# Attention value product: two passes with high and low value parts in one stationary block, instead of three

## The reference, cut to what matters

```python
def one_block(qi):                       # per block of 128 queries
    s = jnp.einsum('bqhd,bkhd->bhqk', qi, k).astype(jnp.float32) * scale
    p = jax.nn.softmax(s, axis=-1).astype(v.dtype)
    return jnp.einsum('bhqk,bkhd->bqhd', p, v)
```

## Time and profile before

| | |
|---|---|
| median of 3 runs | 3137.64 us (3137.29 to 3138.24) |
| the profiled execution's own time | 3137.54 us |
| its span, first to last instruction | 3135.4 us |
| TensorE busy | 3018.9 us (96%), 19892 matmuls |
| VectorE busy | 2122.9 us (68%) |
| ScalarE busy | 1141.8 us (36%) |
| mean granted TensorE clock | 0.982 of full speed |
| attention stages | about 774 to 1057 and 2280 to 2563 us |

### The profile page before, as it was taken

One profiled execution on the slowest core, in us unless ns is written; L12 is line 12 of the kernel. 1 busy time (PEld: TensorE's weight loads), 2 busy tenths in 40 slices (PEclk: granted clock), 3 DMA queues, 4 the chain that ended last, 5 costly groups with the idle time before them and its releaser, 6 DMA issues.

```text
span 3135.4 us, 48664 instructions
## 1 busy us (share of the span) xinstructions
PE 3018.9 (96%) x19892; PEld 2938.2 (94%) x19892; DVE 2122.9 (68%) x3521; ACT 1141.8 (36%) x1820; POOL 85.8 (3%) x164
## 2 busy tenths in 40 slices
PE   7999999998999999999999999999899999999998
PEld 4899999997899999999999999999789999999998
DVE  7666666646655557988968988863565556785675
ACT  3422312422444433434343433442154443443432
POOL 0000000000000000000000000000000000000000
PEclk8999999999999999999999999999999999999999
DMA  8255553345122532444322434334521242122222
GB/s 304 91 202 228 213 190 135 115 153 221 67 75 85 192 112 80 135 141 142 122 95 94 149 121 142 108 114 163 224 82 71 76 186 108 68 95 81 95 68 75
DMA packets 89743, 408.90 MB, mean 130 GB/s; under 512 B 10049, under 2 KB 13569, under 8 KB 68914
## 3 DMA queue, kind: packets, MB, share of 16 engines
q1 hardware_dynamic: 60384, 285.76, 25.6%
q0 software_dynamic: 19872, 94.53, 8.3%
q10 hardware_dynamic: 9266, 25.50, 2.2%
HBM read 359.46 MB, written 46.30 MB: 129 GB/s over the span
## 4 chain that ended last, share of the span: by engine, by line
PE 77%; DVE 14%; ACT 4%; issue 3%; DMA 1%; ACTq 0%; DVEq 0%
PE tile_psum L743 21%; PE misc_psum L860 12%; PE tile_psum L750 11%; PE misc_psum L864 6%; PE tile_psum L1215 6%; PE tile_psum L704 3%; PE tile_psum L1219 3%; PE misc_psum L669 3%; PE tile_psum L669 2%; PE tile_psum L860 2%; PE tile_psum L709 2%; PE tile_psum L1080 1%; DVE h L2254 1%; DVE wlo L2083 1%; PE tile_psum L864 1%
## 5 line engine op out<-in xcount | busy, mean ns | idle before, releaser
L743 PE MATMUL tile_psum<-n_hi,whi 128*128 128x320 f32 x1536 | 352.3, 311 | 4.0 <-issue 2.2
L743 PE MATMUL tile_psum<-n_lo,whi 128*128 128x320 f32 x1536 | 350.1, 309 | 0.0
L2083 DVE TENSOR_TENSOR wlo<-raw,whi 128x2048 fp32r<-128x2048 f32 (+4 forms) x130 | 250.6, 1930 | 114.2 <-ACT whi L1491 112.2
L743 PE MATMUL tile_psum<-x_hi,whi 128*128 128x320 f32 x1300 | 300.1, 312 | 17.4 <-DVE h L2254 11.7
L743 PE MATMUL tile_psum<-x_lo,whi 128*128 128x320 f32 x1300 | 298.3, 311 | 0.0
L743 PEld LDWEIGHTS tile_psum<-n_hi,whi 128*128 128x128 f32 x1536 | 257.6, 189 | 6.8 <-DVE n_lo L2174 4.2
L743 PEld LDWEIGHTS tile_psum<-n_lo,whi 128*128 128x128 f32 x1536 | 258.2, 189 | 0.0
L1491 ACT ACTIVATE whi<-raw 128x2048 fp32r<-128x2048 f32 (+4 forms) x130 | 208.9, 1616 | 126.7 <-DMA raw<-in_w_down 43.7
L1215 PE MATMUL tile_psum<-n_hi,whi 128*128 128x320 f32 x768 | 237.4, 320 | 11.0 <-ACT gate_out L1978 10.3
L2254 DVE SCALAR_TENSOR_TENSOR h<-tile_psum,ada_t,h 128x320 f32<-128x320 f32 (+2 forms) x408 | 154.2, 434 | 129.2 <-PE tile_psum L750 127.5
L750 PE MATMUL tile_psum<-n_hi,wlo 128*128 128x320 f32 x1536 | 241.3, 309 | 0.0
(11 more groups left out here) (384 smaller groups left out, 6450.1 us busy)
## 6 DMA issues: line engine op xcount, KB each, us to landing
w_ada<-in_w_ada POOLq DMA_DIRECT2D x72, 512.0 KB, 4.0
raw<-in_w_up SPq DMA_DIRECT2D x72, 512.0 KB, 3.8
raw<-in_w_up SPq DMA_DIRECT2D x34, 1024.0 KB, 4.9
w_ada<-in_w_ada SPq DMA_DIRECT2D x56, 512.0 KB, 6.3
raw<-in_w_gate SPq DMA_DIRECT2D x24, 1024.0 KB, 4.9
raw<-in_w_down SPq DMA_DIRECT2D x29, 768.0 KB, 4.4
whi<-table_keep SPq DMA_DIRECT2D x20, 1024.0 KB, 4.7
wlo<-table_keep SPq DMA_DIRECT2D x20, 1024.0 KB, 6.9
```

Source lines behind the costliest of these rows:

```text
L743: pe.matmul(tps[:, t.s, m, 0:TH], blk(p, m * n + k)[0], (hi, lo)[b][:, k, tok], start=k == 0 and b == 0, stop=False)
L2083: ins = dve.tensor_tensor(lo_at(r, n)[:, 0:w], raw_at(r, n)[:, 0:w], hi_at(h_, n)[:, 0:w].bitcast(F32), ALU.subtract)
```

## The change

The values are laid out in one tile `v_parts`, for each key tile as four blocks of 64 columns: high of the even head, low of the even head, low of the odd head, high of the odd head. ScalarE and VectorE each write them with two operations of 384 columns instead of one of 768, and VectorE starts after both of ScalarE's. The stationary block of a P is one head's high and low block side by side (128 columns). Two passes follow, one with the high and one with the low part of the probabilities. The result's 64 rows of the high values and 64 rows of the low values have to be added: ScalarE copies the low values' rows to `x_raw` (which lies where `x_lo` lies), moved to the other half of the partitions, VectorE adds the other rows from PSUM, frees the tile, waits for its own write and signals. The split into `x_hi` and `x_lo` is a new entry X h, one step later, at the end of step 5h+7; the last one, X7, ends the list. TensorE waits for `x_split` ahead of the projection. The product now also holds low x low.

```diff
--- before.py
+++ after.py
@@ -266,8 +266,11 @@
             order += [("T", n - 2)] + [("F", 0)] * (n != 2)
             if n % 5 == 1:
                 order += [("P", (n - 2) // 5)]
+            elif n % 5 == 2 and n > 5:
+                order.append(("X", n // 5 - 1))
         if n % 10 == 1 and n < 5 * HEADS:
             order.append(("V", n // 10))
+    order.append(("X", HEADS - 1))
     done, first, fills, out, busy = {}, {}, HYENA_FILLS, [], []
     for at, (what, n) in enumerate(order):
         if what == "F":
@@ -445,7 +448,9 @@
         (krt0,), _ = place(XL, ("k_rope_tmp", [P, TL], F32))
 
         (pth, ptl), _ = place(base, ("probs_t_hi", [P, 5, TL], F32R), ("probs_t_lo", [P, 5, TL], F32R))
-        (vh, vl, krt), _ = place(SM0, ("v_hi", [P, KEYS], F32R), ("v_lo", [P, KEYS], F32R), ("q_rope_tmp", [P, TL], F32))
+        (vals2, krt), _ = place(SM0, ("v_parts", [P, KEYS // P, 4, VD], F32R), ("q_rope_tmp", [P, TL], F32))
+        v_at = [[vals2[:, :, b, :].rearrange("p (a k) v -> p a k v", a=2) for b in bs] for bs in ((0, 3), (1, 2))]
+        (xraw,), _ = place(XL, ("x_raw", [P, 8, T], F32))
         (kh, kl, kh1, kl1, pm, qf, ckh, ckl), end4 = place(
             A0, ("k_hi", [P, KEYS], F32R), ("k_lo", [P, KEYS], F32R), ("k_hi1", [P, KEYS], F32R), ("k_lo1", [P, KEYS], F32R),
             ("probs", [P, 2, T], F32), ("q_f32", [P, T], F32), ("ckv_hi", [P, KEYS], F32R), ("ckv_lo", [P, KEYS], F32R))
@@ -509,6 +514,10 @@
 
             return halves(p) if qt < 4 else p[:, 0:TC]
 
+        def v_psum(m, e):
+
+            return mps[:, m.s, :, 0:KEYS // 2].rearrange("p a (k e v) -> p a k e v", k=3, e=2)[:, :, :, e, :]
+
         def smat(ap, at, n=P):
             return ap[:, at:at + n]
 
@@ -517,6 +526,7 @@
         hi_ready, lo_ready = sem("panel_hi_ready"), sem("panel_lo_ready")
         early_in, piece_in = [sem(f"ada_early_in{k}") for k in range(4)], [sem(f"ada_rows_in{k}") for k in range(2)]
         cols_in, cols_on, turned_out, w3_in = sem("c_cols_in"), sem("c_cols_silu"), sem("ada_turned"), [sem(f"w3_in{l}") for l in range(DEPTH)]
+        x_half, x_sum, x_split, low_values = sem("x_half_out"), sem("x_summed"), sem("x_split"), sem("low_values_part")
         ada_late = [sem(f"ada_late_in{k}") for k in range(2)]
         ada_in, ada_used = [sem(f"ada_in{k}") for k in range(2)], sem("ada_used")
         ada_half = sem("ada_half_done")
@@ -1283,16 +1293,19 @@
                         for t in (turned, vals):
                             pe.wait_ge(t.free, t.free_at)
                         t = taken(slots.head_tile())
+                        both = [vals2[:, kt, n % 2 * 2:n % 2 * 2 + 2, :].rearrange("p b v -> p (b v)") for kt in range(6)]
                         for kt in range(5):
-                            kk = slice((kt + 1) * P, (kt + 2) * P)
-                            mm3([tps[:, t.s, 0, :]], (vh[:, kk], vl[:, kk]), [(pth[:, kt, :], ptl[:, kt, :])], kt == 0, kt == 4)
-                        mm3([tps[:, t.s, 1, 0:TC]], (vh[:, 0:TC], vl[:, 0:TC]), [(pch[:, :], pcl[:, :])], True, True)\
-                            .then_inc(t.done, 1)
+                            for x_ in (pth, ptl):
+                                pe.matmul(tps[:, t.s, 0, :], both[kt + 1], x_[:, kt, :], start=kt == 0 and x_ is pth, stop=kt == 4 and x_ is ptl)
+                        for x_ in (pch, pcl):
+                            ins = pe.matmul(tps[:, t.s, 1, 0:TC], both[0], x_[:, :], start=x_ is pch, stop=x_ is pcl)
+                        ins.then_inc(t.done, 1)
                     elif what == "F":
                         part_of_gate(n)
 
 
                 all_read(tile_free)
+                pe.wait_ge(x_split, HEADS * (l + 1))
                 pe.wait_ge(fill_free, 48 * (l + 1))
                 for m in range(KT):
                     if m % 2 == 0:
@@ -2023,7 +2036,8 @@
                             act.activation(kl1[ROPE_AT[1], :], kl[ROPE_AT[0], :].bitcast(F32), ACT.Copy).then_inc(keys_turned, 1)
                     elif what == "V":
                         m = misc()
-                        split_hi(halves(vh[:, :]), mps[:, m.s, :, 0:KEYS // 2])
+                        for e in range(2):
+                            split_hi(v_at[0][e], v_psum(m, e))
                     elif what == "S":
                         m = misc()
                         c = n % 3
@@ -2039,7 +2053,12 @@
                     elif what == "P":
                         t = seen(slots.head_tile())
                         rows = slice((n % 2) * VD, (n % 2 + 1) * VD)
-                        split_hi(xh[rows, 2 + n // 2, :], flat(tps, t.s)[rows, 0:T])
+                        other = slice((1 - n % 2) * VD, (2 - n % 2) * VD)
+                        act.activation(xraw[rows, 2 + n // 2, :], flat(tps, t.s)[other, 0:T], ACT.Copy).then_inc(x_half, 1)
+                    elif what == "X":
+                        rows = slice((n % 2) * VD, (n % 2 + 1) * VD)
+                        act.wait_ge(x_sum, due(x_sum))
+                        split_hi(xh[rows, 2 + n // 2, :], xraw[rows, 2 + n // 2, :])
                     elif what == "F":
                         after_fill(n)
 
@@ -2881,7 +2900,9 @@
                         lo_part(ql[ROWS[n % 2], n % 2, :], qf[ROWS[n % 2], :], qh[ROWS[n % 2], n % 2, :], q_split)
                     elif what == "V":
                         m = misc()
-                        lo_part(halves(vl[:, :]), mps[:, m.s, :, 0:KEYS // 2], halves(vh[:, :]), m.free)
+                        dve.wait_ge(op_hi, due.now(op_hi) + 2)
+                        for e in range(2):
+                            lo_part(v_at[1][e], v_psum(m, e), v_at[0][e], (low_values, m.free)[e])
                     elif what == "S":
                         scored[n] = m = misc()
                         own(dve.tensor_reduce(stat[:, c:c + 1], scores(m.s, qt), AX.XY if qt < 4 else AX.X, ALU.max))
@@ -2904,7 +2925,14 @@
                     elif what == "P":
                         t = seen(slots.head_tile())
                         rows = slice((n % 2) * VD, (n % 2 + 1) * VD)
-                        lo_part(xl[rows, 2 + n // 2, :], flat(tps, t.s)[rows, 0:T], xh[rows, 2 + n // 2, :], t.free)
+                        dve.wait_ge(x_half, due(x_half))
+                        y = xraw[rows, 2 + n // 2, :]
+                        dve.tensor_tensor(y, y, flat(tps, t.s)[rows, 0:T], ALU.add).then_inc(t.free, 1)
+                        dve.wait_ge(t.free, t.free_at)
+                        dve.sem_inc(x_sum, 1)
+                    elif what == "X":
+                        rows = slice((n % 2) * VD, (n % 2 + 1) * VD)
+                        lo_part(xl[rows, 2 + n // 2, :], xraw[rows, 2 + n // 2, :], xh[rows, 2 + n // 2, :], x_split)
                 dve.sem_inc(heads_done, 1)
                 for m in range(KT):
                     dve.wait_ge(gate_on, due(gate_on))
```

## The result

The changed kernel takes 3143.22 us (median of 20 runs, 3138.86 to 3149.39), the one before 3137.27 in its 20 runs beside it. The ratio is 1.0022, interval [1.0015, 1.0029]: 6.9 us slower by the ratio, 6.0 by the two medians, where I had forecast no change, 3137.6. The time lies in the range (3125 to 3144), but outside the forecast case (3132 to 3142), and the interval excludes 1. The profiled execution took 3142.65 us, its span is 3140.4.

What follows compares the result with a forecast made beforehand. TensorE was taken as the bound, busy nearly all of the span. Removed matmuls -19.8, stage end +3.4, queue stalls +13.4 and clock +3.0 summed to 0.0 us: forecast 3137.6 us, no change, range 3125 to 3144.

Steps and rivals of the forecast that it cites:

- forecast case: Whole kernel: likeliest case, no change at 3137.6 us, own range 3132 to 3142; chance 0.44.
- Removed matmuls, -19.8: Value product: five wide matmuls and one narrow-pass share gone, 1.24 us per head, 9.9 per layer, 19.8 us saved in all.
- The end, +3.4: Layer's last product to projection: added rounding and subtraction lengthen the chain by 1.7 us per layer, 3.4 in all.
- Queue stalls, +13.4: Heads of the attention stage: X and moved half roundings delay TensorE at five places, 6.7 us per layer, 13.4 in both.
- Steps 24 and 29: TensorE's gate matmuls wait for late gate copies: 2.1 us at step 24, 1.7 us at step 29, per layer.
- Steps 9 and 34: TensorE's transposes wait for VectorE's subtraction, delayed by a half roundings' exchange with the split: 0.8 and 1.1 us.
- step 39: Transposes wait for VectorE's subtraction, late by X6 and a half set ahead of it: 1.0 us per layer.
- step 23's maximum: VectorE waits for ScalarE's x_hi ahead of this maximum, which comes 3.35 us late.
- The clock, +3.0: TensorE's clock after new stalls: one fall per layer at 1.5 us, 3.0 in all, bounds 0 and 6.
- rival 3: Two larger stalls and the lengthened end each bring another stretch at 1.2 GHz: slower, 3143.6 us; chance 0.12.
- Rivals 4 and 5: Value product: removed matmuls worth 0.13 us each, 3145.6 (chance 0.01); or weights and passes not changed as said (0.01).
- Rival 1: Attention stage: everything but the end is hidden, -19.8 + 3.4 gives 3121.2 us; chance 0.15.

Runs made afterwards that it cites:

- two passes alone: Kernel before with only the value product's third pass (low values x high probabilities) left out, layout and lists unchanged: 3120.65 us, 0.9949.
- halves back: Changed kernel with half roundings R, R2, L, L2 at the places of the kernel before, X still at the end of step 5h+7: 3141.58 us, 1.0017.
- h late: Changed kernel with GpSimd's load of h issued with the gates of projection block 7 instead of block 3: 3134.88 us, 0.9996.
- X ahead of P: Changed kernel with half roundings at the places of the kernel before and X directly ahead of the next head's value product: 3123.83 us, 0.9964.

## Why the prediction was wrong

**Removed matmuls, -19.8: right.** Stages 10.0 us shorter with two passes alone; the whole 19.8 shows once the wait behind the stage is out of the way.

**The end, +3.4: right.** 1.83 us per layer against 1.7, each part as costed: 0.70, 0.82, 0.73, 0.82. That I counted nothing for the lengthened end was not right: in three of the four ends profiled of the changed kernel the stretch at low clock was 6.8 us long instead of 3.4 and cost 2.6 to 2.8 us of TensorE's work instead of 1.7; behind the fourth there was none.

**Queue stalls, +13.4: right in sum, 6.4 and 6.6 against 6.7 per layer.** Steps 24 and 29 came as worked out (2.50 and 2.15 against 2.1; 1.73 against 1.7), and the waits for the gate copy grew by 4.6 us in layer 0 (3.8 expected). Steps 9 and 34 have 0.5 each in place of 0.8 and 1.1, step 39 only 0.55 in layer 1; smaller waits elsewhere make up for it. VectorE waits 1.21 us for `x_hi` ahead of step 23's maximum, as foreseen. That the sum fits is partly luck: by the same chains 2.1 us per layer were to be left with the halves back, and 6.6 and 7.6 were. The list of differences ahead of the prediction also leaves one out: in step 34 the half L26 now stands ahead of N33, and R2.26 is gone to step 33.

**The clock, +3.0: this step failed.** It said "I count one fall per layer", bounds 0 and 6 us, reasoned from the length of single waits: 1.6 us had kept the full clock, 1.72 had not. In the heads of the changed kernel, behind the stage's start, there are two falls per layer, in both of its profiles and in the one with h late (3.4 us per layer where 1.5 were counted), and more is lost behind the end and behind the wait for `mixed`. Nor did they come where the lengths had put them: 2.50, 2.48 and 2.15 us kept the full clock in the changed kernel, while 1.72 and 1.65 lost it, and twice one of 1.6; with h late the 2.49 us wait lost it and both of 1.6 kept it. The two profiles of the changed kernel lose 8.5 and 15.4 us more to low clock around the stages than the kernel before. Over the whole program every timed run tells it: the mean granted clock is 0.9799 in the 20 runs of the changed kernel and 0.9830 and 0.9828 in two sets of 22 and 27 runs of the one before. One less this clock, times the time, is 63.2 us against 53.3 and 54.0: over 9 us more, as an upper bound, since a low clock costs nothing while TensorE is idle. Without it the change comes out at about zero or a little below. This was rival 3's mechanism, and its 3143.6 is near the 3143.2 measured; but that agreement is luck, since it had no fall at steps 11 and 21, where some came, had one at step 24, and left out the next term.

**A term that was missing, at nothing in the sum.** The longer transfer of h and the wait for `mixed` behind each stage: 0.8 and 2.3 us more in the first profile, 3.2 in all, plus the clock behind it. By the ratios, moving that transfer alone takes 8.2 us off the changed kernel and 1.6 off the one before, so the term is worth some 6.6 us, clock included, with an uncertainty of over 4. The two parts overlap: with h late the changed kernel's mean clock is 0.9819 (10 runs), which is 56.7 us by the same count, so of the 9 us of clock some 6 went with the transfer. I had read the stage and its end, and stopped at the first matmul of the projection.

With these, -19.8 + 3.6 + 13.0 + 3.2 is 0.0, and the clock makes the rest, 6 to 7 us where the sum had 3.0. Rivals 4 and 5 are out: spacing and passes are as forecast. Rival 1, "everything but the end is hidden", needed only X at another place: X ahead of P gives 3123.8, and with the transfer of h moved 3117.8, against its 3121.2.

Not settled: how much of the excess each single fall of the clock makes, since they move from run to run; and by what way one packet of instructions, at that moment, makes a transfer of GpSimd's queue some 1.5 us longer.

## What to carry to other kernels

On engines that take a list in order, put a new piece of work where that engine waits anyway (here ahead of the next value product, 4 us idle), not at the end of a step: with the halves at the same places the same instructions cost 6.6 and 7.6 us per stage or 0.5. When an earlier stage gets shorter, follow the transfers and tiles of the next one too. Price each new wait of TensorE at its length plus 1.7 us of low clock times its chance: by the count above next to nothing up to 1.6 us, over half between 1.63 and 2.8, nearly sure (and up to twice the price) above 3.2. When a chain at a stage's end can't be shortened, reorder one block of the next stage so that independent products come first; turned in every block, the order gave nothing here.

## What the runs showed of the hardware

- The same wait of TensorE is followed by a fall of its clock in one place or execution and not in another, and falls are the more frequent the longer the wait: none in 89 waits of 1.20 to 1.45 us, 3 in 33 of 1.58 to 1.61, 29 in 51 of 1.63 to 2.80, 25 in 26 above 3.2. Behind the same 1.72 us at a stage's end it came in 8 of 14. Each stretch at low clock costs 1.7 us, or twice that. It makes most of the spread: over the timed runs of the kernel before (22 and 27), time and mean granted clock have a correlation of -0.9.
- A 2560 KB transfer issued by GpSimd takes 10.4 to 11.5 us where no packet of the instruction queue q8 starts inside it (later than 0.6 us behind its issue), and 11.9 to 12.7 where one does: 20 and 12 transfers, without exception. At the same place it took 10.7 to 11.5 us with 19892 TensorE instructions and, but for one 11.0, 11.9 to 12.4 with 19796; 96 tiny matmuls bring back the former (11.3 and 10.7). With the transfer or the projection at another place 19796 gave 10.4 to 11.3, and 19892 gave 12.7 once. So it is where the packet falls and not the count; that the packet is the cause is argued, not shown.
- A matmul of 16 columns with its own weights costs 0.11 us, half of one with 512 (0.23).
